# Three edits in a three-branch decoder kernel: weights loaded a phase ahead, gates projected transposed and kept on chip, the last mixer's loop interleaved

## The chip, the cores and the metric

The kernel runs on one core of one Trainium2 chip. The metric is the device time of one execution in microseconds (us), the median over runs.

## What is computed

The reference is one inference step of a two-layer recurrent decoder trunk, for 1024 prompt tokens and for 64 sample tokens (8 requests of 8 tokens, each with its own carried states), model width 1024, all in fp32. Layer 0 holds two mixers (a gated delta rule and an RWKV-7 scan), layer 1 an mLSTM with 8 heads (query and key width 64, value width 128). The change touches the input side of layer 0 and all of layer 1:

```
xn = rms_norm(x, norm1_w);  proj = xn @ w_in1          # q, k (512 each), v, o, z (1024 each), gates
pm  = exp(d - mt) * (q @ k.T)                          # masked decay times scores, per head
num = exp(inter - mt) * (q @ C) + pm @ v               # C, n: matrix memory and normaliser
den = exp(inter - mt) * (q . n) + sum(pm)
h   = num / max(|den|, exp(-mt))
C   = e_c * C + (w_s * k).T @ v;   n = e_c * n + sum(w_s * k)
y   = rms_norm(x + (h * sigmoid(o) * silu(z)) @ w_out1, norm_f_w)
```

Outputs are y for prompt and sample, and the final states of prompt and sample (the sample states have a leading dimension of 8).

## The kernel before

The program is written by hand: each phase is one block in which every engine has its own instruction stream, ordered by semaphores; a phase starts when the one before has ended on all engines. SP issues all DMAs, on one queue. Tokens are tiled by 128 (8 prompt tiles) with one more tile of 64 sample tokens. An fp32 product is made of three TensorE matmuls on split operands (`products`, L82: high times high, high times low, low times high), so every weight block is loaded to SBUF, its high part cast by ACT (`...h`), and its low part subtracted by POOL (`...l`).

The phases, with the prefix that their buffers carry in the trace:

- `phase_norm` (n_, L96): RMSNorm of all tiles, the result turned into x transposed (K.xh, K.xl).
- `phase_gdn_in` (a_, L289): SP loads its weights when the phase starts (L342 to L349), ACT casts (L440, L442), POOL subtracts (L400, L405); PE projects the gates and then 4 groups of 4 column blocks of 128, weights stationary and x moving in pieces of 364, 364 and 360 columns (THIRDS). `over` (L281) runs the body for column block 0, for 1 and 2 in a hardware loop, and for 3.
- `phase_rwkv_in` (b_, L677): the same for the second mixer; its first weights (L725) and parameters (L727 to L730) are loaded when it starts.
- `phase_mix0` (c_, L1053): both mixers of layer 0, the output projection, the next norm. The change leaves it alone.
- `phase_mlstm_in` (e_, L2113): input projection of layer 1 in 16 blocks of 256 columns. The 4 blocks of q and k have the weights stationary. The 12 blocks of v, o and z (L85 to L87 under the loop at L2407) have x stationary and 256 weight columns moving: 9 token tiles times 8 contraction pieces times 3 products, 216 matmuls a block. ACT and DVE make the gate sigmoid(o) * silu(z) in tile GO, and SP stores v, gate and the running maxima (L2209, L2210, L2222, L2223) to scratch in DRAM.
- `phase_mix1` (f_, L2425): one step for each token tile. On PE, in this order: decay logits broadcast to all partitions (L2796, contraction 8), q times k (L2802), decay of the state (L2807), k turned to rows (L2810); then, for the tile before, the gated rows H turned (`end_rows`, L2772) and the output projection of 48 matmuls of 512 columns (`end_project`, L85 to L87); then for this tile the numerators, which alternate two shapes head by head (L2825 pm times v with contraction 128, L2827 q times C with contraction 64), and the state update (`update`, L2763). DVE masks (L2664), multiplies and scales, multiplies H with the gate rows GR that SP loaded, updates C (L2735), adds the residual and norms. Tiles 0 and 1 are written out, 2 to 7 are a hardware loop, and the sample tile comes last, alone: its numerators need each request's own state (L2831, 64 matmuls), its update goes through 8 requests one after the other (`with_batches`), and SP stores each request's states (L2555, L2556). At the phase's start SP loads w_out in 8 pieces, which ACT casts (L2609) and POOL and DVE subtract (L2568, L2710), and while the second tile runs the sample states (L2534, L2535, 32 DMAs).

Of the kernel before, what the change touches and what calls it, by code (L numbers as in the profile page):

```python
# [95 lines left out]
def phase_norm(nc, K, x_prompt, x_sample, shift, norm_w, p_shift, s_shift):  # L96

    with ExitStack() as ctx:
# [13 lines left out]
        with nc.Block() as block:  # L112
            @block.sync
            def _(sp):
# [3 lines left out]
                with sp.Fori(0, TILES // 2 - 1) as g:  # L118
                    for b in range(2):
                        sp.wait_ge(norm, 2 * g + b + 1)  # L120
                        sp.dma_start(x[:, b, :], x_prompt[0, bass.ds((2 * g + b + 2) * P, P), :]).then_inc(x_in[b], 16)
# [167 lines left out]
def phase_gdn_in(nc, K, w_in, conv_w, conv_state, a_log, dt_bias, S, p_conv, s_conv):  # L289


    with ExitStack() as ctx:
        sb = lambda n, s: ctx.enter_context(nc.sbuf_tensor("a_" + n, s, F32))
        sem = Events(nc, ctx, "a_")
        W = [sb(f"w{m}", [P, KT, P]) for m in range(4)]
        parts = lambda n, s: [ctx.enter_context(nc.sbuf_tensor(f"a_{n}{h}", s, F32R)) for h in "hl"]
        WP = [parts(f"wp{m}", [P, KT, P]) for m in range(4)]
        wg = sb("wg", [P, KT, 2 * AH])
# [9 lines left out]
        rows = sb("rows", [64, AQKV])  # L308
# [5 lines left out]
        gp = sb("gp", [P, 2, AH])  # L314
# [20 lines left out]
        halo, tailed, tails_t, tails_kept, tails_out, par, par2, pre_t, pre_k, gates, gate_a, gate_v, padded, dseq, pseq = [sem(n) for n in (  # L335
            "halo", "tailed", "tails_t", "tails_kept", "tails_out", "par", "par2", "pre_t", "pre_k", "gates", "gate_a",
            "gate_v", "padded", "dseq", "pseq")]

        with nc.Block() as block:
            @block.sync  # L340
            def _(sp):
                sp.dma_start(W[0][:, :, :], w_block(w_in, 0, P)).then_inc(w_ld[0], 16)  # L342
                sp.dma_start(cw_rows[:, :], conv_w).then_inc(par, 16)
                sp.dma_start(cs_rows[:, :], conv_state.rearrange("b r c -> (b r) c")).then_inc(par, 16)
                sp.dma_start(wg[:, :, :], w_block(w_in, AGATE, 2 * AH)).then_inc(par, 16)
                sp.dma_start(gp[:, 0, :], as_row(a_log)).then_inc(par2, 16)
                sp.dma_start(gp[:, 1, :], as_row(dt_bias)).then_inc(par2, 16)
                for m in range(1, 4):
                    sp.dma_start(W[m][:, :, :], w_block(w_in, m * AKEY, P)).then_inc(w_ld[m], 16)  # L349

                def load(m, j):
                    sp.wait_ge(low[m], j + 1)
                    alone(sp, K)
                    sp.dma_start(W[m][:, :, :], w_block(w_in, m * AKEY + (j + 1) * P, P)).then_inc(w_ld[m], 16)

                def body(j, more):
                    for m in range(3):
                        if more:
                            load(m, j)
# [11 lines left out]
                    if more:  # L371
                        load(3, j)
# [15 lines left out]
            def _(pool):  # L388
# [21 lines left out]
                def body(j, more):  # L410
# [7 lines left out]
                    for m in range(3):  # L418
# [8 lines left out]
                        if more:  # L427
                            split(m, j + 1)
                    if more:
                        split(3, j + 1)  # L430
# [3 lines left out]
            def _(act):  # L434
                def split(m, j):

                    act.wait_ge(w_ld[m], 16 * (j + 1))
# [3 lines left out]
                act.wait_ge(par, 48)  # L441
# [12 lines left out]
                act.wait_ge(par2, 32)  # L454
# [40 lines left out]
                def body(j, more):  # L495
                    keep(0, j)
                    if more:
                        split(0, j + 1)
                    keep(1, j)
                    if more:  # L500
                        split(1, j + 1)
# [3 lines left out]
                    if more:  # L505
                        split(2, j + 1)
# [18 lines left out]
                    if more:  # L525
                        split(3, j + 1)
# [3 lines left out]
            def _(dve):  # L530
# [9 lines left out]
                dve.wait_ge(par2, 32)  # L540
# [57 lines left out]
            def _(pe):  # L598
                pe.wait_ge(par, 48)
# [74 lines left out]
                over(pe, AH, body)  # L674


def phase_rwkv_in(nc, K, w_in, mu, w0, w2, a0, a2, k_k, k_a, r_k, S):  # L677

    with ExitStack() as ctx:
# [40 lines left out]
        with nc.Block() as block:  # L722
# [58 lines left out]
            def _(act):  # L781
# [20 lines left out]
                for m in range(4):  # L802
                    split(m, 0)
# [2131 lines left out]
```

## Time and profile before

| | |
|---|---|
| median of 3 runs | 2180.28 us (2179.63 to 2193.6) |
| the profiled execution | 2189.03 us, its span 2187.2 us |
| mean granted TensorE clock | 0.907 of full |
| busy: PE / DVE / ACT / POOL | 1921.7 / 891.8 / 576.8 / 445.2 us |
| a_ phase, b_ phase | 72.5 to 308.7 us with its gates before, 308.7 to 607 us |
| c_ phase | 607 to 1378 us |
| e_ phase | 1378 to 1838.6 us |
| f_ phase | 1838.6 to 2187.2 us |

PE is TensorE's matmuls, PEld its weight loads, DVE VectorE, ACT ScalarE, POOL GpSimd, SPq the queue of SP. A matmul on fp32 operands leaves several records in the trace: an fp32 matmul of the f_ phase (numerators, scores) two, a product on split operands one each. PEclk is the granted TensorE clock as a share of full speed, 1.00 for 2.4 GHz and 0.50 for 1.2 GHz. A record's duration is that of one instruction from its start to its modelled end; consecutive matmuls overlap, so the pace is read from start to start.

### The profile page before, as it was taken

Reading aid. Unit: us, or ns where it says so; the run is one execution under the profiler, and the core shown is the slowest. Engines: PE = TensorE matmul, PEld = TensorE weight load, DVE = VectorE, ACT = ScalarE, POOL = GpSimd, SP = SyncE. Lnnn points to the kernel's source line nnn. Section 1 sums busy time; section 2 is a strip of 40 time slices with the busy share of each in tenths; the row PEclk is TensorE's granted clock in tenths of the full one; section 3 lists DMA queues with packets and bytes.
Section 4 is the critical chain, followed back from the end, with each engine's and each line's share of the span. In section 5 each row is a group of like instructions: output and inputs, shape, how many; then the busy total and the mean of one; then the engine's idle time right before and its main releaser. Section 6 shows DMA issues by size and latency. Waiting matters only on the chain. (4 is left out here: it accounts for less than half of the span.)

```text
span 2187.2 us, 33920 instructions
## 1 busy us (share of the span) xinstructions
PE 1921.7 (88%) x13387; PEld 1663.1 (76%) x13387; DVE 891.8 (41%) x1709; ACT 576.8 (26%) x1171; POOL 445.2 (20%) x444
## 2 busy tenths in 40 slices
PE   3999968999779999999999889499999996999985
PEld 2799858889668767776776666399999995777764
DVE  4255534655556546645654543320001102533432
ACT  4344432333323223323232112321111111211101
POOL 2322111112054234324333200221111110100000
PEclk9999989999879999999999786799999997688887
DMA  4122131331161112211231101522131113522215
GB/s 122 43 81 80 52 91 40 101 101 42 52 224 49 50 39 67 73 37 53 67 91 35 31 30 48 155 80 80 60 99 41 60 61 125 147 79 65 91 49 44
DMA packets 192189, 160.54 MB, mean 73 GB/s; under 512 B 34563, under 2 KB 174060, under 8 KB 192089
## 3 DMA queue, kind: packets, MB, share of 16 engines
q1 hardware_dynamic: 192088, 159.12, 25.1%
q8 instruction: 73, 1.20, 0.2%
q14 instruction: 28, 0.22, 0.0%
HBM read 103.96 MB, written 55.14 MB: 73 GB/s over the span
## 5 line engine op out<-in xcount | busy, mean ns | idle before, releaser
L1809 PE MATMUL c_banks<-c_wo,c_ot 128*128 128x512 f32 (+1 forms) x288 | 131.7, 612 | 0.5 <-ACT c_invt L1410 0.5
L2369 DVE SCALAR_TENSOR_TENSOR e_t<-e_t,e_bank 128x512 f32<-128x512 f32 (+1 forms) x20 | 12.7, 633 | 287.9 <-ACT e_t L2321 287.9
L85 PE MATMUL e_bank<-e_wp0h,e_xh 128*128 128x256 f32 x432 | 122.5, 283 | 1.5 <-issue 1.5
L85 PE MATMUL e_bank<-e_wp1h,e_xh 128*128 128x256 f32 x432 | 122.3, 283 | 0.0
L86 PE MATMUL e_bank<-e_wp1l,e_xh 128*128 128x256 f32 x432 | 122.3, 283 | 0.0
L87 PE MATMUL e_bank<-e_wp0h,e_xl 128*128 128x256 f32 x432 | 122.3, 283 | 0.0
L86 PE MATMUL e_bank<-e_wp0l,e_xh 128*128 128x256 f32 x432 | 122.3, 283 | 0.0
L87 PE MATMUL e_bank<-e_wp1h,e_xl 128*128 128x256 f32 x432 | 122.2, 283 | 0.0
L1350 POOL TENSOR_TENSOR c_m<-c_sc,c_lev 128x256 f32<-128x256 f32 (+1 forms) x118 | 97.7, 836 | 55.5 <-DVE c_sc L1657 52.8
L1809 PEld LDWEIGHTS c_banks<-c_wo,c_ot 128*128 128x128 f32 (+1 forms) x288 | 53.0, 189 | 67.5 <-issue 65.8
L1709 DVE TENSOR_TENSOR c_inv<-c_inv,c_banks 128x128 f32<-128x128 f32 (+1 forms) x252 | 59.0, 278 | 97.3 <-PE c_banks L1930 96.4
L1350 POOL TENSOR_TENSOR c_m<-c_nt,c_lev 128x256 f32<-128x256 f32 (+1 forms) x59 | 46.7, 792 | 252.7 <-DVE c_nt L1626 126.0
L85 PEld LDWEIGHTS e_bank<-e_wp0h,e_xh 128*128 128x128 f32 x432 | 82.9, 192 | 1.7 <-issue 1.7
L85 PEld LDWEIGHTS e_bank<-e_wp1h,e_xh 128*128 128x128 f32 x432 | 82.9, 192 | 0.0
L86 PEld LDWEIGHTS e_bank<-e_wp1l,e_xh 128*128 128x128 f32 x432 | 82.9, 192 | 0.0
L87 PEld LDWEIGHTS e_bank<-e_wp1h,e_xl 128*128 128x128 f32 x432 | 82.9, 192 | 0.0
L86 PEld LDWEIGHTS e_bank<-e_wp0l,e_xh 128*128 128x128 f32 x432 | 82.9, 192 | 0.0
L87 PEld LDWEIGHTS e_bank<-e_wp0h,e_xl 128*128 128x128 f32 x432 | 82.9, 192 | 0.0
L1908 PE MATMUL c_banks<-c_inv,c_m 128*64 128x64 f32 (+1 forms) x1008 | 60.5, 245 | 20.0 <-POOL c_m L1350 20.0
L1908 PEld LDWEIGHTS c_banks<-c_inv,c_m 128*64 128x64 f32 (+1 forms) x1008 | 42.7, 146 | 45.9 <-issue 30.1
L1930 PEld LDWEIGHTS c_banks<-c_y 64*128 64x128 f32 (+1 forms) x1008 | 67.7, 211 | 8.1 <-issue 8.0
L1930 PE MATMUL c_banks<-c_y 64*128 64x64 f32 (+1 forms) x1008 | 73.8, 300 | 0.0
(570 smaller groups left out, 5166.7 us busy)
## 6 DMA issues: line engine op xcount, KB each, us to landing
e_w<-in_w_in_dram SPq DMA_DIRECT2D x16, 1024.0 KB, 6.5
b_w<-in_w_in_dram SPq DMA_DIRECT2D x17, 512.0 KB, 6.4
scratch_rw<-b_x SPq DMA_DIRECT2D x16, 544.0 KB, 2.7
a_w<-in_w_in_dram SPq DMA_DIRECT2D x16, 512.0 KB, 5.8
c_rw<-scratch_rw SPq DMA_DIRECT2D x32, 256.0 KB, 2.9
scratch_qkv<-a_o SPq DMA_DIRECT2D x12, 544.0 KB, 4.7
e_xs<-scratch_xnT SPq DMA_DIRECT2D x8, 544.0 KB, 4.0
scratch_ql<-e_qb SPq DMA_DIRECT2D x8, 544.0 KB, 2.9
```

The source lines that it names most:

```text
L85: pe.matmul(out, w[0], x[0], start=first, stop=False)
L86: pe.matmul(out, w[0], x[1], start=False, stop=False)
L87: return pe.matmul(out, w[1], x[0], start=False, stop=last)
L1350: pool.tensor_tensor(M[u][0:T, :, 0:T // 2].rearrange("p k (b h) -> p k b h", h=1 << l), late(src, l, T), bc(lev[0:T, l:l + 1, 0:T // 2].r ...
L1709: dve.tensor_tensor(x, x, z, ALU.subtract).then_inc(ev(f"xd{u}"), 1)
L1809: mm = pe.matmul(bank[6 + c][0:T, :], OT[:, kt, 0:T], wo[:, kt, 512 * c:512 * c + 512], start=(kt == 0), stop=(kt == KT - 1))
L1908: mm = pe.matmul(y_at(u, T, k), M[u][0:T, k, 0:T // 2], half(X[u][0:T, k, :], l, T, 0), start=True, stop=True)
L1930: mm = pe.matmul(z_all(u, T, e)[:, p, :], XC[u][r, p, 0:T], Y[u][r, p, 0:T // 2], start=True, stop=True)
L2369: dve.scalar_tensor_tensor(out=t2, in0=t2, scalar=1.0, in1=two(b, at), op0=ALU.add, op1=ALU.mult).then_inc(ev(f"free{b}"), 1)
```

## The change

**Weights a phase ahead.** The weight and parameter buffers of a_ and b_ become shared ones (K.W, K.WP, K.rows, K.wg, K.gp, K.lora). a_'s are loaded by SP during `phase_norm`, between the x tiles. In the last column block of a_, SP loads b_'s first blocks into the same buffers, and ACT and POOL split them there; b_ projects its first blocks without a wait for weights.

```
                 sp.dma_start(x[:, n % 2, :], x_prompt[0, (n + 2) * P:(n + 3) * P, :]).then_inc(x_in[n % 2], 16)
+                if n == 1:
...
+                if n >= 2:
+                    sp.dma_start(K.W[n - 2][:, :, :], w_block(w_in0, (n - 2) * AKEY, P)).then_inc(K.a_w[n - 2], 16)
...
+                    if more:
+                        sp.dma_start(W[m][:, :, :], w_block(w_in, m * AKEY + (j + 1) * P, P)).then_inc(w_ld[m], 16)
+                    else:
+                        sp.dma_start(W[m][:, :, :], w_block(w_in, ACOLS + (m if m else 4) * BW, P)).then_inc(K.b_w[m], 16)
...
-                    if more:
-                        load(3, j)
+                    load(3, j, more)
```

The SP queue at the end of a_'s last column block, before, from the last store of q, k, v to b_'s first loads (a_z is the gate z, a_o are the projected columns, a_tails the last rows of the convolution):

```order
L362 DMA scratch_qkv<-a_o 128x1088
L367 DMA scratch_z<-a_z 128x8x128
L370 DMA scratch_z<-a_z 64x128
L376 DMA scratch_qkv<-a_o 128x1088 x2
L380 DMA out_p_conv_dram<-a_tails 9x1x128
L382 DMA out_s_conv_dram<-a_tails 72x1x128
L339 UNCONDITIONAL_BRANCH
L723 UNCONDITIONAL_BRANCH
L725 DMA b_w<-in_w_in_dram 128x8x128
```

and now:

```order
L358 DMA k_w<-in_w_in_dram 128x8x128 x3
L365 DMA scratch_qkv<-a_o 128x1088
L370 DMA scratch_z<-a_z 128x8x128
L373 DMA scratch_z<-a_z 64x128
L358 DMA k_w<-in_w_in_dram 128x8x128
L378 DMA scratch_qkv<-a_o 128x1088 x2
L382 DMA out_p_conv_dram<-a_tails 9x1x128
L384 DMA out_s_conv_dram<-a_tails 72x1x128
L343 UNCONDITIONAL_BRANCH
L720 UNCONDITIONAL_BRANCH
```

Three of b_'s first four blocks now stand ahead of a_'s last stores, the fourth behind those of z, and a_ ends only when it has been loaded and split.

**Gates transposed.** In e_, the 4 blocks of v come first, in the old form. The 8 blocks of o and z then have the weights stationary and x moving in THIRDS; the gate is written to K.G ([128, 8, 1088], transposed, on chip), so scratch g, tile GO, its stores and the loads of GR in f_ are gone. The stores of the running maxima move up behind the q and k blocks. Small buffers share space (QB lies on xs, li and lf on VB, bc_ is K.u).

```
-                with pe.Fori(0, ROUNDS) as g:
-                    for p in range(6):
+                with pe.Fori(0, V_BLOCKS // 2) as g:
...
+                with pe.Fori(0, OZ_BLOCKS // 2) as g:
+                    for p in range(2):
...
+                        for i in range(6):
+                            t, (at, n) = i // 3, THIRDS[i % 3]
+                            pe.wait_ge(ev(f"free{i}"), 2 * g + p + BEFORE_OZ[i])
+                            for kt in range(KT):
+                                w = [x[:, kt, t * P:(t + 1) * P] for x in WP[p]]
+                                mm = products(pe, bank[i][:, 0:n], w, [x[:, kt, at:at + n] for x in X], kt == 0, kt == KT - 1)
```

**The last mixer.** All loops of f_ are written out over 9 steps, and the sample tile is the fifth (`SLOT = 4`). In step k, PE does the numerators of k (8 matmuls pm times v, then 8 q times C), the update of k, half of the projection of k-1, the scores of k+1 (L2857 to L2872), the other half, and the turn of k. H is turned ungated; DVE multiplies by K.G behind the turn (`gate`, into OG), then ACT casts and DVE subtracts. XR, the residual rows, has two buffers; the first wait of DVE in f_, for the final norm's weights (`ld_nw`, loaded at L2528), moves behind step 0. The sample's numerators are 64 matmuls with contraction 64 in alternating row halves; its 8 request updates stand between the matmuls of the two projection halves, four in each. SP loads the sample states in 4 DMAs after step 0's loads and stores them in 8 DMAs in step 5.

```
+                scores(0)
+                for k in range(STEPS):
+                    numerators(k)
+                    if k != SLOT:
+                        pe.wait_ge(ev("og"), 2 * k)
...
+                        update(P, KW, EARLY, "upd")
...
+                    if k >= 1:
+                        project(k - 1, 0, early)
+                    if k + 1 < STEPS:
+                        scores(k + 1)
+                    if k >= 1:
+                        project(k - 1, 1, late)
+                    turn(k)
+                project(STEPS - 1, 0)
+                project(STEPS - 1, 1)
...
+                        if k == SLOT:
+                            sp.wait_ge(ev("upd_s"), DB)
+                        else:
+                            sp.wait_ge(ev("upd"), prompts(k + 1))
+                        load_v(k + 1)
...
+                    if k == SLOT + 1:
+                        store_states(0)
+                        store_states(DB // 2)
```

PE in a tile of f_ before (f_ut and f_et are decay rows, f_ql q and k, f_h the rows H, f_woh and f_wol w_out's parts, f_oth and f_otl those of the turned rows, f_va v, f_pm masked scores, f_c the state, f_kw scaled keys); the three projection rows stand 16 times, the two numerator rows 8 times:

```order
L2796 MATMUL f_bank<-f_ut,k_sel 128x128 x8
L2802 MATMUL f_bank<-f_ql 128x128 x8
L2807 MATMUL f_bank<-f_et,k_sel 128x128 x4
L2810 MATMUL f_bank<-k_ident,f_ql 128x128 x4
L2772 MATMUL f_bank<-k_ident,f_h 128x128 x8
L85 MATMUL f_bank<-f_woh,f_oth 128x512
L86 MATMUL f_bank<-f_wol,f_oth 128x512
L87 MATMUL f_bank<-f_woh,f_otl 128x512
...
L2825 MATMUL f_bank<-f_va,f_pm 128x129
L2827 MATMUL f_bank<-f_c,f_qe 128x129
...
L2763 MATMUL f_bank<-f_va,f_kw 64x129 x8
```

and now, from a step's numerators to its turn; the projection rows stand 8 times in each half:

```order
L2833 MATMUL f_bank<-f_va,f_pm 128x129 x8
L2839 MATMUL f_bank<-f_c,f_qe 128x129 x8
L2816 MATMUL f_bank<-f_va,f_kw 64x129 x8
L85 MATMUL f_bank<-f_woh,f_oth 128x512
L86 MATMUL f_bank<-f_wol,f_oth 128x512
L87 MATMUL f_bank<-f_woh,f_otl 128x512
...
L2857 MATMUL f_bank<-f_ut,k_sel 128x128 x8
L2862 MATMUL f_bank<-f_ql 128x128 x8
L2869 MATMUL f_bank<-f_et,k_sel 128x128 x4
L2872 MATMUL f_bank<-k_ident,f_ql 128x128 x4
...
L2883 MATMUL f_bank<-k_ident,f_h 128x128 x8
```

The numerators of one shape now stand together, the scores lie between two projection halves, and the turn is followed by numerators and update of the next tile rather than by the projection that needs its result.

## Rows read from the trace of the kernel before

**Rows 1.** Busy time by stage of e_ and f_: stretch, length, busy time and records of each engine, clock, DMA share.

```profile
1512.70:1838.60 325.90, 311.66 (x2596) 311.24 (x2594) 25.70 (x42) 52.99 (x71) 50.83 (x11) 0.98 0.20 62
...
1866.00:2081.00 215.00, 202.43 (x1016) 160.49 (x1015) 90.33 (x216) 32.39 (x91) 5.50 (x7) 0.81 0.31 89
2081.00:2108.30 27.30, 21.16 (x97) 16.09 (x97) 8.47 (x19) 3.27 (x14) 0.60 (x2) 0.87 0.18 58
2108.30:2171.50 63.20, 51.85 (x372) 40.54 (x372) 26.93 (x70) 8.06 (x19) 1.05 (x2) 0.77 0.34 44
2171.50:2187.20 15.70, 0.00 (x0) 0.00 (x0) 0.00 (x0) 0.00 (x0) 0.00 (x0) 0.50 0.81 46
```

**Rows 2.** PE in one tile of the f_ loop: start, length, engine, line, operands, records, [idle before].

```profile
1958.56 0.49 PE L2825 MATMUL f_bank<-f_va,f_pm 128*128 128x129 f32 x2
...
1958.98 0.49 PE L2827 MATMUL f_bank<-f_c,f_qe 64*128 64x129 f32 x2
...
1962.73 1.10 PE L2763 MATMUL f_bank<-f_va,f_kw 128*64 128x129 f32 x16
1963.77 2.05 PE L2796 MATMUL f_bank<-f_ut,k_sel 8*128 8x128 f32 x16
1965.74 1.16 PE L2802 MATMUL f_bank<-f_ql 64*128 64x128 f32 x16
1967.82 1.74 PE L2807 MATMUL f_bank<-f_et,k_sel 8*128 8x128 f32 x8 [0.92 <-DVE f_c L2735]
...
1970.58 1.94 PE L2772 MATMUL f_bank<-k_ident,f_h 128*128 128x128 f32 x8
...
1973.41 0.79 PE L85 MATMUL f_bank<-f_woh,f_oth 128*128 128x512 f32 x1 [0.89 <-DVE f_otl L2639]
...
1978.57 0.40 PE L85 MATMUL f_bank<-f_woh,f_oth 128*128 128x512 f32 x1
...
1986.97 0.38 PE L2825 MATMUL f_bank<-f_va,f_pm 128*128 128x129 f32 x2
```

**Rows 3.** The view of group 1, for pieces of that tile and the start of f_.

```profile
1968.10:1978.20 10.10, 9.21 (x31) 7.24 (x30) 5.49 (x14) 2.25 (x3) 0.00 (x0) 0.50 0.30 98
...
1838.60:1886.00 47.40, 38.50 (x157) 31.09 (x158) 23.23 (x44) 12.94 (x24) 10.92 (x6) 0.50 0.67 201
```

**Rows 4.** The timeline at the start of f_ and in its sample tile.

```profile
1849.99 2.16 DVE L2664 SCALAR_TENSOR_TENSOR f_dm<-f_bank,f_wt,k_lcausal 128x128 f32<-128x128 f32 x8 [22.80 <-DMA f_nw<-in_norm_f_w_dram]
...
2135.22 1.97 PE L2831 MATMUL f_bank<-f_cb,f_ws 128*64 128x129 f32 x16
```

**Rows 5.** The timeline at the end of e_.

```profile
1825.60 0.28 PE L87 MATMUL e_bank<-e_wp1h,e_xl 128*128 128x256 f32 x1
...
1838.69 0.41 SPq L2483 DMA_DIRECT2D f_ql<-scratch_ql  x1
```

**Rows 6.** PE in a_, eighteen moving matmuls of 364 and 360 columns apart.

```profile
285.95 0.32 PE L85 MATMUL a_bank<-k_xh,a_wp3h 128*128 128x364 f32 x1
...
288.93 0.33 PE L85 MATMUL a_bank<-k_xh,a_wp3h 128*128 128x360 f32 x1
```

**Rows 7.** The timeline from the norm to a_'s first product with weights.

```profile
46.47 0.43 SPq L342 DMA_DIRECT2D a_w<-in_w_in_dram  x1
...
53.12 0.26 ACT L442 ACTIVATE a_wgph<-a_wg 128x64 fp32r<-128x64 f32 x1 [8.84 <-DMA a_wg<-in_w_in_dram]
...
56.54 0.58 PE L85 MATMUL a_bank<-k_xh,a_wgph 128*8 128x512 f32 x1 [1.04 <-POOL a_wgpl L400]
```

**Rows 8.** The timeline from a_ to b_.

```profile
302.18 1.52 SPq L376 DMA_DIRECT2D scratch_qkv<-a_o  x2
...
308.82 0.41 SPq L725 DMA_DIRECT2D b_w<-in_w_in_dram  x1
...
312.80 1.06 ACT L801 ACTIVATE b_wp0h<-b_w 128x1024 fp32r<-128x1024 f32 x1 [13.68 <-DMA b_w<-in_w_in_dram]
...
316.42 0.64 PE L85 MATMUL b_bank<-k_xh,b_wp0h 128*128 128x364 f32 x1 [2.43 <-POOL b_wp0l L768]
```

More of the change, by code:

```diff
@@ L965, in project @@
                     b0 = 3 * (m % 2)
-                    pe.wait_ge(high[m], k + 1)
-                    pe.wait_ge(low[m], k + 1)
+                    if not (isinstance(k, int) and k == 0):
+                        pe.wait_ge(high[m], k)
+                        pe.wait_ge(low[m], k)
                     for g, (c, n) in enumerate(THIRDS):
@@ new lines, in _ @@
+                act.wait_ge(ev("turned"), 2)
+                for k in range(V0, OZ0):
+                    high(k + 1)
+                    act.wait_ge(ev("out_v"), 32 * (k - V0))
+                    for i, at in enumerate(PAIRS):
+                        b = V_PLACES[k % 2][i]
+                        r, n = at[2], slice(at[0], at[0] + at[1])
+                        act.wait_ge(ev("bank_full"), done_at(k, i))
+                        act.activation(VB[0:r, n, :], two(b, at), ACT.Copy).then_inc(ev(f"free{b}"), 1)
@@ L2683, in tile @@
+                    dve.wait_ge(ev("rows"), k + 1)
                     if T == P:
@@ new lines, in _ @@
+                dve.wait_ge(ev("ld_nw"), 16)
+                for k in range(STEPS):
+                    if k >= 2:
+                        add(k - 2, 1)
+                    if k >= 1:
+                        gate(k - 1)
+                    if k >= 2:
+                        scale(k - 2)
+                    if k >= 1:
+                        low(k - 1)
+                    if k >= 2:
+                        norm(k - 2)
+                    if k >= 1:
+                        rows_out(k)
+                        if k == SLOT:
+                            for b in range(DB // 2):
+                                states(b, EARLY)
+                        else:
+                            state(k)
+                        add(k - 1, 0)
+                    if k + 1 < STEPS:
+                        scores(k + 1)
+                    if k == SLOT:
+                        for b in range(DB // 2, DB):
+                            states(b, LATE)
@@ L2758, in _ @@
+                add(STEPS - 2, 1)
+                gate(STEPS - 1)
+                scale(STEPS - 2)
+                low(STEPS - 1)
+                norm(STEPS - 2)
+                add(STEPS - 1, 0)
+                add(STEPS - 1, 1)
+                scale(STEPS - 1)
+                norm(STEPS - 1)
             @block.tensor
@@ L2790, in tile, with sample_update @@
-                def tile(i, T, last):
-                    n = i + 1
-                    kept = i if T != P else i - 1 if not isinstance(i, int) or i > 0 else 0
-                    pe.wait_ge(ev("ut"), n)
-                    pe.wait_ge(ev("ot_low"), 2 * kept)
-                    for h in range(CH):
-                        mm = pe.matmul(v4(h // 4, T, T)[:, h % 4, :], K.sel[:, h, 0:T], ut[:, 0:T], start=True, stop=True)
+                def sample_update(b, banks):
+                    pe.wait_ge(ev("pick"), b + 1)
+                    if b % 4:
+                        pe.wait_ge(ev("cb"), b)
+                    update(SR, KM[b % 4], banks, "upd_s")
@@ L2797, in tile, with scores @@
+                def scores(k):
+                    T = order[k][2]
+                    pe.wait_ge(ev("ut"), k + 1)
+                    pe.wait_ge(ev("hr"), k)
+                    for h in range(CH):
+                        mm = pe.matmul(v4(6 + h // 4, T, T)[:, h % 4, :], K.sel[:, h, 0:T], ut[:, 0:T], start=True, stop=True)
                     mm.then_inc(ev("ub"), 1)
-                    pe.wait_ge(ev("hr"), i)
-                    pe.wait_ge(ev("ld_q"), 32 * n)
+                    pe.wait_ge(ev("ld_q"), 32 * (k + 1))
```

818 lines of the change are left out of this document (407 added, 411 removed).

## The prediction

> **What bounds the kernel now.** I read the busy time by stage first, then PE's timeline in one tile of the last mixer, then the seams between phases. In every long stage PE is the busiest engine: 311.7 of 325.9 us in e_, 202.4 of 215.0 us in the tile loop of f_, where DVE has 90.3 and ACT 32.4 us [rows 1]. So a step costs what PE needs for it, at the clock that it is granted. That clock is 0.98 of full in e_, but 0.81 in f_'s loop, 0.77 in its sample tile, and f_ ends with 15.7 us in which no engine works and only stores run [rows 1].
>
> One tile of f_ takes 215/7 = 30.7 us [rows 1]. By starts [rows 2]: numerators 16 pairs of records of 0.42 us, 6.7 us; update 1.04; scores 6.8, with a wait of 0.92 in it; turn 2.8, with a wait of 0.89; projection 13.56. From 1968.1 to 1978.2 the granted clock is 0.50 [rows 3], the lower of its two levels (1.2 GHz): it falls after the light scores and the first wait, and comes back only well inside the projection. From 1978.57 to 1986.97 the last 36 of its 48 matmuls take 8.40 us, 0.233 each; the 12 before took 5.16, 0.43 each [rows 2].
>
> **A, weights a phase ahead.** From the first load of a_ to the cast of its gate weights pass 53.12 - 46.47 = 6.65 us, and all behind that cast stays [rows 7]: at most 6.7 us are gained. The loads (four blocks of 0.5 MB, 2.1 MB) now run between the norm's x tiles; at the 201 GB/s of a stretch full of loads [rows 3] they need 10.4 us of DMA. If they held the norm for all of that, this would be a loss of 3.7; if they fit in its pauses, a gain of 6.7. I take +3. At the other seam, 316.42 - 308.82 = 7.6 us from b_'s first load to its first product go [rows 8]. But SP issues the fourth block's load behind z's stores, about 302; such a block is there 4.0 us after its issue (308.82 to 312.80), and cast and subtracted 3.6 us later (316.42) [rows 8]: about 309.5 to 311, and a_ ends behind that rather than at 308.8. I take +4 of 0 to 7.6. A: +7, between -4 and 14.
>
> **B, gates transposed.** The 12 blocks in the old form run from 1512.7 [rows 1] to 1825.88 [rows 5]: 26.1 us a block of 216 matmuls of 256 columns. A moving matmul of 364 columns takes (288.93 - 285.95)/18 = 0.1656 us [rows 6], so a block of 144 takes 23.8: 8 x 2.3 = 18 us, all of it on PE, which has no waits there (311.7 of 313.2 busy). The end of e_ is 1838.69 - 1825.88 = 12.8 us of two gate steps, the stores of gate and maxima and their landing [rows 5]; without stores I leave 2.8 us for the gate steps: +10 (bounds 5 and 12). The first block of v uses two banks that ACT and DVE have just filled into w and em: -1.5 (0 to -3). DVE's and ACT's work per block has the same number of elements, and has a block's 24 us to be done in. B: +26.5, between 20 and 29.
>
> **C, the last mixer.** A steady step of the new order, at full clock, from [rows 2]: turn 1.0 (1.94 at half clock); numerators 3.4; update 1.04; scores 1.97 + 1.16 + half of the 2.76 us that the decay and row matmuls take at half clock, 4.5, with 0.4 for hand-overs; projection 48 x 0.233 = 11.2; another 0.5 for hand-overs (between 0 and the 1.8 us of waits that the tile has now). Sum 22.0 us against 30.7.
>
> The numerators are the term that no row shows. Alternating the contraction 128 and 64, a record takes 0.21 us [rows 2]. Records of one shape take less: 1.97 us for the 16 of the sample's numerators, 0.12 each [rows 4], and 0.0725 for the scores in alternating row halves [rows 2], which is how the new q times C is laid out. So 16 x 0.12 + 16 x (0.0725 to 0.12) = 3.1 to 3.8, and 6.7 if grouping does nothing; I take 3.4, by the row of one shape.
>
> The Trainium skill, "TensorEngine Tiling (Array Packing)", section "Key Properties", says that changing the tiling mode, not only the tile, drains TensorE. By that rule the alternation pays at each of 16 switches and the grouped form at one or two; the 0.21 against 0.12 us agrees with it, and the sum would stay as it is.
>
> DVE does not become the bound: 90.3 us over 7 tiles is 12.9, ACT's 4.6 [rows 1]; even one after the other that is 17.5 of 22.0 us. What waits for what: the turn's result passes DVE (gate), ACT (high), DVE (low) while PE does the next tile's numerators and update (4.4 us), which is close; a shortfall of 0.5 is in the hand-overs. The masked scores are made under the second projection half (5.6 us).
>
> The steps, from [rows 1 to 4] where not said. Step 0: DVE's first mask waited until 1849.99 for the norm's weights [rows 4], 11 us into f_; that wait is gone and all behind it is some 6 us earlier, but the 8 casts of w_out and DVE's share of them still stand before step 1's scores, at half clock: 32.5. Step 1, cold with its first projection: 28. Steps 2, 3, 5, 6, 7: 5 x 22.0 = 110. Step 4: own numerators 1.9, 128 records of the states at 0.0725 to 0.12 (9 to 15, taken as 11), 8 updates of 1.04, projection 11.2, scores 4.9, turn 0.5: 38; then step 5 can load v only when the last update has read it, 4 us as for a block [rows 8]: 42. Step 8, without scores: 17. The end: gate, high, square, low with PE idle, a projection begun cold, add, norm, store: 26, nearly as the 27.3 us of the last prompt tile now [rows 1], since the store's landing is added and the next tile's part is not. Last, 3 us of low clock behind that 4 us wait, 3 for loads that queue behind the sample states' stores (15.7 us of stores at 0.81 of the DMA engines now [rows 1]), and 8 for some falls of the clock in the scores. Sum 32.5 + 28 + 110 + 42 + 17 + 26 + 14 = 269.5, against 2187.2 - 1838.7 = 348.5: +79. Bounds 45 and 105, by the rivals below.
>
> **Sum.** 7 + 26.5 + 79 = 112.5 us. The profiled execution took 2189.0 us (its span 2187.2 and 1.8 around it), so the same would read 2076.5. The median of the runs is 8.75 us lower, and the parts that differ are not in the edits: 2068 us.
>
> **Rivals.** First, the clock falls in every step (20%). For it: it does so in each tile now, after 4 us of light scores and a wait [rows 2, 3]. Against it: now 11 us of numerators, update and scores go before the fall, where the new order has at most 5.5 us between two halves of dense projection. Price: scores 1 us longer and the half behind them 2.4 us (12 matmuls at 0.43 rather than 0.233), 3.4 x 8 = 27, of which 8 are in the sum: 2087 us.
> The Trainium skill, "TensorE: Matmul & The Clock Gate", section "HAM oscillation — how this bites in real kernels", describes a kernel whose short bursts of matmuls are parted by gaps, and which starts each burst at the low clock. By that rule this rival would hold; the trace agrees so far for gaps behind light work [rows 2, 3] and does not show how it is without the gap.
>
> Second, all better (14%): no fall of the clock, no queueing, the wait for v hidden: 18 us of the 269.5 go, and the weights cost the norm nothing, 6 more: 2044 us.
>
> Third, grouping does nothing for the numerators (9%): 3.3 x 8 = 26: 2094 us. Against it stand the two faster rows above.
>
> Fourth, the hand-overs bind (6%): DVE, ACT and DVE between turn and projection take over 4.4 us, say 4 us more a step, 7 x 4 = 28: 2096 us. For it: three engines in a row, with the norm of an older tile in DVE's stream between them.
>
> Fifth, the other side (3%): the clock never comes up in f_. For it: in its first 47.4 us the granted clock is 0.50 although PE is busy for 38.5 of them [rows 3], and it is now dense projection of 13.6 us in one piece that raises it; halves of 5.6 us may not. A step at half clock is 2 x 21.5 + 0.5 = 43.5 us; seven of them 150 more and the sample 32 more, less the 14 above: 2068 + 168 = 2236 us. It decides once the clock stays down in more than six of the eight steps (134 us, the 112 gained and 1%, over 21.5 each).
>
> **How the numbers follow.** The forecast has 48%. A change of 1% (22 us) is about what a measurement of this kernel can tell from none. All cases but the fifth lie below 2158, and half clock in five or six steps would land near 2180: faster 0.96, same 0.02, slower 0.02. The range goes from 2036, with A and B at their upper ends on the second rival, to 2106, with the third or fourth rival and A at a loss; it leaves out the fifth and sums of two rivals.
>
> **What would show it.** Right: f_ of 255 to 285 us with steps of 21.5 to 24 us; numerators at 3.1 to 3.8 us; granted clock near 1.00 in the projection halves of steps 2, 3, 6, 7; no idle end of over 5 us; 23.8 us for a block of o or z; b_'s first product within 2 us of its phase's start, and a_ longer by 2 to 4. Wrong: a step of over 25 us, a clock of 0.5 in half of each step, the norm longer by over 5 us, or PE idle before the first projection half by more than 1 us in every step.

## The result, and the profile after

The changed kernel takes 2063.91 us, the median of 4 runs (2059.42 to 2072.46); the kernel before beside it took 2181.25 us. The ratio is 0.9446, with a 95% interval of 0.9412 to 0.948: 5.5% faster. The forecast was 2068, in a range from 2036 to 2106.

The profiled execution took 2063.12 us against 2189.03 before. Its busy times by phase (columns as in [rows 1]; the norm, a_, b_, c_, e_, f_, cut where each phase's first DMA is issued):

```profile
0.00:47.35 47.35, 16.24 (x72) 12.89 (x72) 23.92 (x37) 20.79 (x37) 13.44 (x47) 0.72 0.51 155
47.35:308.01 260.66, 232.89 (x1353) 213.49 (x1353) 121.81 (x143) 110.24 (x167) 62.25 (x64) 0.96 0.23 68
308.01:599.85 291.84, 253.06 (x1370) 236.40 (x1370) 150.56 (x137) 91.46 (x179) 35.23 (x18) 0.93 0.21 70
599.85:1365.76 765.91, 692.98 (x5778) 544.12 (x5778) 408.16 (x1004) 208.59 (x533) 235.57 (x277) 0.91 0.22 63
1365.76:1796.78 431.02, 407.93 (x2682) 400.93 (x2682) 57.42 (x75) 92.82 (x130) 80.62 (x24) 0.98 0.24 71
1796.78:2061.40 264.62, 233.21 (x1556) 191.80 (x1556) 134.78 (x326) 50.93 (x133) 19.73 (x15) 0.83 0.44 103
```

Against the same cuts of before (46.5, 262.4, 299.5, 769.3, 461.0, 348.5 us; c_ starts there with its first load at 608.3) the phases changed by +0.9, -1.7, -7.7, -3.4, -30.0 and -83.9 us: A 8.5 (forecast 7), B 30.0 (26.5), C 83.9 (79), and 3.4 in c_, which no edit touches.

The same view in finer pieces: the last two blocks of e_ work (v, then o and z), e_'s end, and in f_ step 0, steps 1 to 3, the sample's step 4, steps 5 to 7, step 8 with the final projection, and the last store:

```profile
1498.62:1602.40 103.78, 103.78 (x866) 103.78 (x865) 0.29 (x2) 18.01 (x23) 18.45 (x4) 1.00 0.28 79
1602.40:1794.20 191.80, 191.80 (x1154) 191.50 (x1152) 29.79 (x46) 35.23 (x55) 32.20 (x7) 1.00 0.13 39
1794.20:1796.78 2.58, 0.00 (x0) 0.00 (x0) 1.06 (x2) 0.47 (x1) 0.00 (x0) 1.00 0.00 0
1796.78:1831.12 34.34, 24.27 (x144) 21.58 (x145) 22.86 (x42) 12.14 (x21) 11.43 (x6) 0.58 0.92 263
1831.12:1895.09 63.97, 63.97 (x446) 53.61 (x445) 39.44 (x101) 11.05 (x37) 1.86 (x2) 0.96 0.39 99
1895.09:1938.81 43.72, 40.05 (x374) 32.14 (x373) 21.22 (x62) 10.25 (x23) 0.93 (x1) 0.88 0.07 22
1938.81:2018.79 79.98, 74.47 (x444) 60.07 (x445) 36.57 (x94) 11.46 (x37) 3.11 (x3) 0.81 0.63 108
2018.79:2057.20 38.41, 30.46 (x154) 24.41 (x152) 14.70 (x30) 6.02 (x15) 2.40 (x3) 0.88 0.15 48
2057.20:2061.40 4.20, 0.00 (x0) 0.00 (x0) 0.00 (x0) 0.00 (x0) 0.00 (x0) 0.50 0.31 127
```

The 8 blocks of o and z take 191.80 us, 24.0 each, where a block took 26.1 [rows 1, 5], and e_ ends 2.6 us behind its last matmul, not 12.8. In f_ the reader sees PE busy for 63.97 of 63.97 us in steps 1 to 3, with clock 0.96; then less in steps 4 to 7, where the clock is 0.88 and 0.81 and PE stands idle for 9 us. The idle end of 15.7 us [rows 1] is now 4.2.

One step, that of tile 2, on PE (as [rows 2]; L2883 is the turn, L2833 and L2839 the numerators, L2816 the update, L2857 to L2872 the scores; the projection halves stand where the lines are left out):

```profile
1852.14 1.03 PE L2883 MATMUL f_bank<-k_ident,f_h 128*128 128x128 f32 x8
1853.01 1.95 PE L2833 MATMUL f_bank<-f_va,f_pm 128*128 128x129 f32 x16
1854.89 1.16 PE L2839 MATMUL f_bank<-f_c,f_qe 64*128 64x129 f32 x16
1855.98 1.10 PE L2816 MATMUL f_bank<-f_va,f_kw 128*64 128x129 f32 x16
...
1862.81 2.05 PE L2857 MATMUL f_bank<-f_ut,k_sel 8*128 8x128 f32 x16
1864.78 1.16 PE L2862 MATMUL f_bank<-f_ql 64*128 64x128 f32 x16
1865.88 1.15 PE L2869 MATMUL f_bank<-f_et,k_sel 8*128 8x128 f32 x8
1866.96 0.87 PE L2872 MATMUL f_bank<-k_ident,f_ql 128*128 128x128 f32 x4
...
1874.63 1.04 PE L2883 MATMUL f_bank<-k_ident,f_h 128*128 128x128 f32 x8
1875.50 1.95 PE L2833 MATMUL f_bank<-f_va,f_pm 128*128 128x129 f32 x16
```

From 1853.01 to 1855.98 the numerators take 2.97 us, against 6.7 in [rows 2]: the 16 records of pm times v keep the pace of the sample's [rows 4], those of q times C that of the scores. The step is 22.5 us long. It has no wait, and yet two speeds: from the last records of the scores (row 1866.96) on, PE runs slower for a while. The granted clock around that place, and in the same place of step 7 (columns as before):

```profile
1862.81:1866.50 3.69, 3.69 (x38) 3.45 (x38) 2.30 (x8) 0.00 (x0) 0.00 (x0) 1.00 0.12 48
1866.50:1870.50 4.00, 4.00 (x16) 3.30 (x16) 3.20 (x8) 1.06 (x1) 0.00 (x0) 0.60 0.29 66
1870.50:1875.50 5.00, 5.00 (x26) 4.07 (x26) 0.60 (x1) 0.00 (x0) 0.00 (x0) 0.98 0.00 0
...
2006.54:2012.00 5.46, 5.46 (x32) 4.82 (x32) 4.08 (x13) 1.06 (x1) 0.00 (x0) 0.56 0.00 0
```

PE is busy in every microsecond of these windows. The clock falls inside the scores of step 7 and at the very end of those of step 2 (it stands at 0.50 from 1867.26 to 1870.67), and comes back inside the second projection half.

What PE waited for in steps 5 and 6, and SP's queue ahead of the second wait:

```profile
1938.81 3.69 PE L2833 MATMUL f_bank<-f_va,f_pm 128*128 128x129 f32 x16 [3.56 <-DMA f_va<-scratch_v]
...
1981.83 2.08 PE L2862 MATMUL f_bank<-f_ql 64*128 64x128 f32 x16 [5.51 <-DMA f_ql<-scratch_ql]
...
1956.14 5.91 SPq L2534 DMA_DIRECT2D out_s_n_dram<-f_cb  x1
1962.10 3.86 SPq L2532 DMA_DIRECT2D out_s_c_dram<-f_cb  x1
1965.99 4.80 SPq L2534 DMA_DIRECT2D out_s_n_dram<-f_cb  x1
1970.91 2.82 SPq L2497 DMA_DIRECT2D f_ql<-scratch_ql  x1
```

The first wait is for v behind the sample's last update, as forecast. The second is for q and k of the next tile: SP issued that load only at 1970.91, since the eight stores of the sample states, issued from 1946.9 on, took its time until then, some of them 4 to 6 us to issue.

The seams: a_'s first gate product (56.54 before [rows 7]), the cast of b_'s fourth block, and b_'s first product (316.42 before [rows 8]):

```profile
50.76 0.58 PE L85 MATMUL a_bank<-k_xh,a_wgph 128*8 128x512 f32 x1 [1.04 <-POOL a_wgpl L402]
...
297.93 1.04 SPq L358 DMA_DIRECT2D k_w<-in_w_in_dram  x1
...
303.42 1.06 ACT L445 ACTIVATE k_wp3h<-k_w 128x1024 fp32r<-128x1024 f32 x1 [8.54 <-DMA k_w<-in_w_in_dram]
...
308.28 0.67 PE L85 MATMUL b_bank<-k_xh,k_wp0h 128*128 128x364 f32 x1
```

### The profile page after: what moved, and what is told of

Same layout as the page of the kernel before. It is cut to its first block and busy times, and to the rows that moved or that the text cites. A ratio compares the mean times of both kernels' runs of the same rounds, so it can differ in the third digit from the quotient of the medians.

```text
span 2061.4 us, 32418 instructions
## 1 busy us (share of the span) xinstructions
PE 1836.3 (89%) x12811; PEld 1599.6 (78%) x12811; DVE 896.7 (43%) x1722; ACT 574.8 (28%) x1179; POOL 446.8 (22%) x444
## 5 line engine op out<-in xcount | busy, mean ns | idle before, releaser
L2368 DVE SCALAR_TENSOR_TENSOR e_t2m<-e_t2m,e_bank 128x364 f32<-128x364 f32 (+1 forms) x24 | 12.8, 532 | 265.1 <-ACT e_t2m L2320 265.1
L85 PE MATMUL e_bank<-e_xh,e_wp0h 128*128 128x364 f32 (+1 forms) x288 | 94.7, 329 | 3.6 <-POOL e_wp0l L2250 3.6
L86 PE MATMUL e_bank<-e_xl,e_wp0h 128*128 128x364 f32 (+1 forms) x288 | 94.6, 329 | 0.0
L86 PE MATMUL e_bank<-e_xl,e_wp1h 128*128 128x364 f32 (+1 forms) x288 | 94.6, 329 | 0.0
L87 PE MATMUL e_bank<-e_xh,e_wp0l 128*128 128x364 f32 (+1 forms) x288 | 94.6, 329 | 0.0
L87 PE MATMUL e_bank<-e_xh,e_wp1l 128*128 128x364 f32 (+1 forms) x288 | 94.6, 329 | 0.0
L85 PE MATMUL e_bank<-e_xh,e_wp1h 128*128 128x364 f32 (+1 forms) x288 | 94.5, 328 | 0.0
L2250 POOL TENSOR_TENSOR e_wp0l<-e_w,e_wp0h 128x2048 fp32r<-128x2048 f32 x8 | 36.8, 4595 | 159.1 <-ACT e_wp0h L2263 159.1
L2250 POOL TENSOR_TENSOR e_wp1l<-e_w,e_wp1h 128x2048 fp32r<-128x2048 f32 x8 | 38.7, 4837 | 147.2 <-ACT e_wp1h L2263 147.2
L85 PE MATMUL f_bank<-f_woh,f_oth 128*128 128x512 f32 (+1 forms) x144 | 63.9, 444 | 3.8 <-DVE f_otl L2677 3.8
L1445 ACT ACTIVATE c_y<-c_banks 128x128 f32<-128x128 f32 (+1 forms) x126 | 34.7, 275 | 111.2 <-PE c_banks L1900 110.3
L872 DVE TENSOR_TENSOR b_x<-b_u 128x1024 f32<-128x1024 f32 x16 | 19.6, 1224 | 96.4 <-ACT b_us L784 96.4
```

Source lines behind the costliest of these rows:

```text
L85: pe.matmul(out, w[0], x[0], start=first, stop=False)
L86: pe.matmul(out, w[0], x[1], start=False, stop=False)
L87: return pe.matmul(out, w[1], x[0], start=False, stop=last)
L1445: act.activation(Y[u][0:T, 0:2, 0:T // 2], y_all(u, T), ACT.Copy).then_inc(ev(f"y{u}"), 1)
L2250: pool.tensor_tensor(WP[b][1][:, :, :], W[b][:, :, :], WP[b][0][:, :, :].bitcast(F32), ALU.subtract).then_inc(ev(f"low{b}"), 1)
```

## The experiments

All are the changed kernel but for the edit shown; the ratio is to the kernel before, run beside each. The length of f_ is that of the profiled execution. Of the variants, the alternating numerators, the projection in one piece and the last two rows have a ratio clear of the changed kernel's interval; the others overlap with it. f_ alone scatters too: three profiles with the same code in f_ (changed, again, A undone) have 264.6, 273.4 and 267.3 us, most of the difference in one wait for q and k in step 6 (5.5, 13.1 and 11.1 us). So a smaller difference is read from the step in which it arises.

| run | ratio (95%) | f_, us |
|---|---|---|
| changed kernel | 0.9446 (0.9412 to 0.948) | 264.6 |
| changed kernel again | 0.9445 (0.9418 to 0.9473) | 273.4 |
| A undone | 0.9521 (0.9475 to 0.9567) | 267.3 |
| numerators alternate | 0.9598 (0.9568 to 0.9629) | 300.4 |
| projection in one piece | 0.9518 (0.9483 to 0.9552) | 282.1 |
| state stores spread | 0.9396 (0.936 to 0.9431) | 259.4 |
| scores cut up | 0.9496 (0.9464 to 0.9527) | 264.0 |
| step 0 of DVE turned | 0.9423 (0.9388 to 0.9459) | 259.4 |
| sample tile last | 0.9482 (0.9446 to 0.9519) | 266.1 |
| all edits | 0.9403 (0.935 to 0.9457) | 252.1 |
| all, cut up outside the sample only | 0.9315 (0.9293 to 0.9337) | 242.2 |
| the same, q times C first in step 5 | 0.9314 (0.929 to 0.9338) | 246.0 |

**A undone.** The three functions of the norm, a_ and b_ are put back.

> The norm, a_ and b_ phases are those of before; e_ and f_ are those of the changed kernel. If the early loads are worth what the seams show (a_'s first gate product at 50.8 rather than 56.5 us, b_'s first product at 308.3 rather than 316.4), c_ starts 8.5 us later than in the changed kernel and the time is 8 to 9 us longer, with f_ unchanged at about 264.6 us. Rival: the loads only move, what the seams gain is lost in the norm and at the end of a_; then under 3 us.

The ratio is 0.0075 higher, but the intervals touch, and in the profile c_, the same code, took 779.7 us rather than 765.9. By the phases, c_ starts at 604.0 us, against 599.9 in the changed kernel and 608.3 before, which runs the same code up to there. In the seven other runs with A as it is, c_ started between 598.4 and 600.3. So A is worth 4 to 10 us, and the rival falls; no closer, since the two executions without A differ by 4.3 us with the same code.

**Numerators alternate.**

```
-                    for h in range(CH):
...
+                        for h in (0, 2, 4, 6, 1, 3, 5, 7):
+                            r = slice(64 * (h % 2), 64 * (h % 2) + 64)
+                            pe.matmul(at(h), PM[0:T, h, 0:T], VA[0:T, h, :], start=h not in (2, 3, 4, 5), stop=False, skip_group_check=True)
+                            mm = pe.matmul(at(h), qe[r, h // 2, :], C[r, h // 2, :], start=False, stop=True, skip_group_check=True)
```

> The numerators of a prompt tile alternate head by head between contraction 128 and 64 again, all else as in the changed kernel. If the alternation itself costs (0.21 us a record against 0.09 in the grouped form), a step's numerators take 6.6 rather than 3.0 us: 3.6 us x 8 steps, 29 us longer, perhaps 2 to 3 less where they hide a wait. Rival: the grouped form is fast because nothing waits around it, not for its shape; then 0 to 5 us.

f_ is 35.8 us longer. The numerators of step 6 on PE, the first pair, the last record and the update behind it:

```profile
1994.96 0.39 PE L2837 MATMUL f_bank<-f_va,f_pm 128*128 128x129 f32 x2
1995.28 0.49 PE L2838 MATMUL f_bank<-f_c,f_qe 64*128 64x129 f32 x2
...
2001.13 0.49 PE L2838 MATMUL f_bank<-f_c,f_qe 64*128 64x129 f32 x2
2001.54 1.10 PE L2816 MATMUL f_bank<-f_va,f_kw 128*64 128x129 f32 x16
```

From 1994.96 to 2001.54 are 6.58 us, at full clock, for the same 32 records: 3.6 more a step, 29 in eight. Undoing the grouping brings the long numerators back. The edit also takes the heads in the order of before, so that four products q times C in a row lie in the same row half; what that alone costs was not run. Sixteen records of contraction 64 in one row half, the sample's pm times v in the changed kernel, take 1.98 us at full clock, 0.9 more than the 1.09 of q times C in alternating halves:

```profile
1895.09 1.98 PE L2833 MATMUL f_bank<-f_va,f_pm 64*64 64x129 f32 x16
```

So some 0.9 of the 3.6 us may be the order of heads (an estimate from these rows); the rest is the alternation of shapes. The other 7 us are the net of uneven steps: the sample's is 1.7 us shorter, and step 1 alone is 13.4 longer. Its busy time here, and in the changed kernel (columns as in [rows 1]):

```profile
1834.90:1870.20 35.30, 35.30 (x151) 27.41 (x150) 11.11 (x31) 3.23 (x11) 0.00 (x0) 0.66 0.37 73
...
1831.12:1853.01 21.89, 21.89 (x150) 18.60 (x150) 11.16 (x30) 3.23 (x11) 0.00 (x0) 0.95 0.60 119
```

Both steps begin at the low clock behind the idle time of step 0. With grouped numerators it comes up 1.0 to 4.1 us behind their start in step 1, in all eleven profiles that have them; with alternating ones only 17.4 us behind it, inside the projection's first half, though PE is busy throughout: 35.3 us at a mean clock of 0.66 against 21.9 at 0.95.

**Projection in one piece.**

```
                         project(k - 1, 0, early)
+                    if k >= 1 and k != SLOT:
+                        project(k - 1, 1, late)
                     if k + 1 < STEPS:
                         scores(k + 1)
-                    if k >= 1:
-                        project(k - 1, 1, late)
```

> In steps 1 to 3 and 5 to 8 both projection halves stand together before the scores of the next tile, as one piece of 11.2 us. My theory: the second half covers the chain mask 2.15, exp 1.06, masked scores 1.28, scaled keys 0.68 and their hand-overs, some 6 us behind the scores; without it the turn waits for the scaled keys, 5 to 6 us in each of 6 steps (the last has no scores): 30 to 36 us longer. Rival: the halves matter for the clock alone, which one long dense piece brings up better; then equal or up to 10 us shorter.

f_ is 17.4 us longer, its prompt steps 26.2 to 26.9 us; half of what I expected, and of the sign that the rival excluded. Numerators and turn of step 2:

```profile
1854.81 3.64 PE L2833 MATMUL f_bank<-f_va,f_pm 128*128 128x129 f32 x16
...
1879.65 1.94 PE L2883 MATMUL f_bank<-k_ident,f_h 128*128 128x128 f32 x8 [1.99 <-DVE f_kw L2734]
```

The wait is 1.7 to 2.0 us in the prompt steps, not 6 (5.5 in step 3, whose scores are the sample's): DVE's chain starts behind the first group of the scores, and the rest of them, 3.4 us here, covers its first half. What else the step lost is clock. It falls in the scores, and stays at 0.50 through the wait, the turn and the numerators behind it (pm times v 3.64 us rather than 1.95); before the change it stayed there through the turn and the first 12 matmuls of the projection. So the halves cover DVE's chain. That they also help the clock, by dense work soon behind the light, is argued from these rows and not shown by a run of its own.

**State stores spread.**

```
-                    if k == SLOT + 1:
-                        store_states(0)
-                        store_states(DB // 2)
+                    if k > SLOT:
+                        store_states((k - SLOT - 1) // 2 * (DB // 2), (k - SLOT - 1) % 2)
```

> The sample states are stored by one pair of DMAs in each of the steps 5 to 8, rather than by all eight in step 5. My theory: the wait of 5.5 us for q and k in step 6 is SP's queue standing behind those stores (24 us of issue); it goes, and with it part of the low clock behind it: 6 to 9 us shorter, and no wait of over 1 us for a load in steps 6 to 8. Rival: the stores' issue time only moves, and the last stores or a later load wait instead: no change, or longer at the end.

f_ is 5.3 us shorter, a little less than expected, step 6 takes 24.0 us rather than 30.3, and PE has no wait for a load in steps 6 to 8. The ratio is lower, but its interval overlaps with the changed kernel's. The stores' issue does not only move: in steps 6 and 7 a store now takes 0.8 to 1.2 us to issue, where it had taken up to 5.9. What the wait is worth differs by execution: it was 5.5 us in the changed kernel's profile and 13.1 in that of its repeat, where f_ took 273.4 us.

**Scores cut up.** The scores' function is split in three; the first part stays, the second goes behind 6 matmuls of the second half, the third behind 12.

> The scores no longer stand in one piece: their first group (decay logits, 2.0 us) stays between the projection halves, q times k goes behind the first 6 of the 24 matmuls of the second half, decay and rows behind the next 6. My theory: the clock falls in the piece of 4.8 us of matmuls of contraction 8 and 64; cut up it stays at full, and the four or five steps that fall in the changed kernel lose 3 us less each: 9 to 15 us shorter, prompt steps of 21 us. Rival: matmuls of contraction 8 and 64 let the clock fall wherever they stand, or each change of shape costs; then no change or up to 10 us longer.

f_ did not change, and the ratio is if anything worse. So I missed the total, but not for the rival's reason alone: steps 2, 5 and 7 took 21.3 to 22.9 us rather than 22.5 to 25.7, and steps 3 and 4, around the sample, lost it again with 22.8 and 48.6 rather than 19.6 and 43.7. Where the clock holds, cutting up costs 0.4 us a step (21.3 against the 20.9 below). Nor does it always hold: in steps 2, 5, 6 and 7 it fell from the scores on in 17 of the 20 steps of the five profiles with whole scores (changed, again, A undone, states spread, step 0 turned), and in 4 of the 16 of the four profiles with cut-up ones.

**Step 0 of DVE turned.** `scores(1)` goes ahead of the subtractions of w_out's pieces 5 and 7.

> In step 0 DVE makes tile 1's masked scores before its last two subtractions of w_out rather than behind them. My theory: the turn of step 0 waits 5.5 us for the scaled keys because DVE stands behind the casts; it goes 4 us earlier and all behind it: 4 us shorter. Rival: the first projection then waits for those two subtractions: no change.

f_ is 5.2 us shorter in the profile; the turn of step 0 waits 1.83 us instead of 5.47, and the first projection starts behind the update without a wait. In the ratio, 0.9423, so little cannot be told from none.

**Sample tile last.** `SLOT = 8`, the state stores behind the last prompt tile's.

> The sample tile is the last of the 9 steps rather than the fifth; its state stores stand at the end. My theory: its own work stays woven in either way; what the middle costs now is the wait of 3.6 us for v, that of 5.5 us for q and k behind the state stores and some 2 us of low clock behind them, 11 us; what the end would cost is some 10 us of state stores that nothing covers. So -5 to +8 us. Rival: the middle is worth the whole idle end of the kernel before, 15.7 us: 12 us longer or more.

+1.5 us in f_. No step waits for a load, and in steps 5 and 6 the clock holds; step 5, all of it:

```profile
1926.20:1947.12 20.92, 20.92 (x151) 17.64 (x150) 12.84 (x33) 4.18 (x13) 0.93 (x1) 1.00 0.32 102
```

What that gains goes into the stores at the end: the last of them is issued at 2044.61 and the sample's y behind it at 2047.73. The fifth place by itself is worth nothing measurable; with the stores spread, f_ is 7 us shorter than with the sample last.

**All edits.** States spread, scores cut up, step 0 turned, b_'s fourth block loaded ahead of z's stores, and DVE's subtraction ahead of the norm's scale at the end.

> States stored over steps 5 to 8, scores cut up, step 0 of DVE turned, b_'s fourth weight block loaded ahead of z's stores, and at the end the subtraction ahead of the norm's scale. If the causes add up: 5 (stores, measured) + 9 to 15 (clock) + 4 (step 0) + 2 (a_) + 1 (end) = 21 to 27 us shorter than the changed kernel. If the rival on the clock holds: 8 to 12.

f_ is 12.5 us shorter and a_ 2.7 us: 15 of the 21 to 27 us expected, more than the 8 to 12 of the rival. c_, unedited, was 10 us longer in this profile, and the runs lie between 2046 and 2069 us. PE's waits in the profile name what is left:

```profile
1903.50 1.06 PE L2890 MATMUL f_bank<-k_ident,f_h 128*128 128x128 f32 x8 [2.65 <-DVE f_kw L2734]
...
1939.68 1.98 PE L2817 MATMUL f_bank<-f_va,f_ws 64*64 64x129 f32 x16 [3.18 <-DVE f_cb L2765]
```

Behind the cut-up scores of the sample, the turn waits for DVE's scaled keys; in the sample's step its late updates wait for the states.

**Cut up outside the sample only.**

```
+                    whole = k in (0, SLOT - 1, SLOT)
+                    if whole:
+                        scores_qk(k + 1)
+                        scores_rest(k + 1)
```

> As the run with all edits, but the scores are cut up only in steps whose neighbours are prompt tiles: the sample's own scores and those made beside its late updates stand in one piece again. My theory: cut up, the rest of the scores comes late where DVE has the sample's four extra products to make or where the late updates take the places, and PE waits for the scaled keys; step 3 goes from 22.8 to 19.6 us and step 4 from 48.4 to 42 to 44, so f_ from 252 to about 244 us and the whole is 18 to 22 us below the changed kernel. Rival: those steps are long for the clock alone; then f_ stays at 250 to 253.

242.2 us in f_, and 2039.8 us in all beside 2068.2 of the changed kernel (2036 to 2043 against 2063 to 2079): 28 us less, with one more variant the best of this study, 6.9% below the kernel before. Step 3 took 19.6 us as expected, step 4 only came down to 45.4. No run has all the other edits with whole scores, so what cutting up gives by itself is read from the steps alone: steps 2, 5, 6 and 7 together took 86.6 us here and 95.0 with the states spread and whole scores. A prompt step on PE, between its numerators and the next, and its clock:

```profile
1842.90 1.95 PE L2834 MATMUL f_bank<-f_va,f_pm 128*128 128x129 f32 x16
...
1852.70 2.05 PE L2858 MATMUL f_bank<-f_ut,k_sel 8*128 8x128 f32 x16
...
1856.27 1.16 PE L2866 MATMUL f_bank<-f_ql 64*128 64x128 f32 x16
...
1858.95 1.15 PE L2876 MATMUL f_bank<-f_et,k_sel 8*128 8x128 f32 x8
...
1863.34 1.04 PE L2890 MATMUL f_bank<-k_ident,f_h 128*128 128x128 f32 x8
1864.21 1.95 PE L2834 MATMUL f_bank<-f_va,f_pm 128*128 128x129 f32 x16
```

```profile
1842.90:1864.21 21.31, 21.31 (x150) 17.47 (x149) 12.74 (x33) 4.17 (x13) 0.93 (x1) 1.00 0.29 87
1906.00:1920.00 14.00, 14.00 (x74) 10.92 (x75) 6.16 (x19) 1.06 (x1) 0.00 (x0) 0.54 0.01 1
```

21.31 us, all of it busy, at full clock; the step of the changed kernel that had the same work took 22.5 to 25.7. In the sample's step the clock still falls.

**q times C first in step 5.**

> As the run before it, but in the step behind the sample the 8 matmuls q times C stand ahead of the 8 pm times v, so that they run while v is loaded. They take 1.1 to 2.2 us: the wait of 3.6 us for v gets that much shorter, 1 to 2 us in all. Rival: the sample's last update is what ends last there, not the load; then nothing.

The wait for v is 1.99 rather than 3.75 us, as expected, steps 4 and 5 together took 67.1 rather than 68.1 us, and the time is the same: 2039.45 us. What it gains is under what the runs can tell: f_ is 3.7 us longer in this profile, in which the clock fell in steps 2 and 6, whose code is that of the run before.

**The changed kernel again.**

> The changed kernel again, as it is, to stand beside the two variants on one chip: its ratio to the kernel before is 0.941 to 0.948, f_ 262 to 267 us.

The ratio is as expected; f_ in the profile is 273.4 us, outside what I had written, mostly for the wait named above (7.6 us more of it). Its clock fell in step 1 as well (23.1 us), where the first profile had none.

## Why the prediction was right

The total was 112.5 us less by the forecast, 117.3 by the medians. Part of that closeness is luck. Profile against profile it was 125.9 us, 13.4 more than forecast: 1.5 in A, 3.5 in B, 4.9 in C and 3.4 in c_, which no edit touches. The profiled execution of before lies 7.8 us above the median of its runs, that of now 0.8 below, so the medians come closer to the forecast than the parts do. By the prediction's steps:

- **What bounds.** PE at its granted clock: steps 1 to 3 have no idle time on PE at all. The 0.5 us for hand-overs was too much; gate, cast and subtraction fit behind numerators and update, and the fourth rival, that they bind, has no row for it.
- **A.** The first seam gained 5.8 us at a_'s first product, the norm's 0.9 already taken off: +3 was low, for the loads fit into the norm's pauses (the norm took 45.9 to 47.5 us in the eleven executions with them, 45.5 and 46.5 without). The second gained 8.1 - 5.8 = 2.3 (forecast 4): the fourth block's load, issued at 297.93, was there 5.5 us later rather than 4.0, and a_ ended behind it. Loading it ahead of z's stores took 3 to 4 us more off a_ (256.7 to 257.9 in three runs, against 260.2 to 261.7). The mechanism was right, its two halves mis-sized in opposite directions.
- **B.** 8 x (26.1 - 24.0) = 17 of the 18 forecast, and 10.2 of 10 at the end. The 1.5 us of waiting for two banks did not come: v starts at 1498.62 with no wait. The rest is 0.6 us in the v blocks, and 1.5 in the q and k blocks and 0.8 at e_'s start, which no edit explains; in the q and k blocks of before the clock stood at 0.50 for 3.4 us (1415.21 to 1418.62), and now it does not. No run undoes B by itself: its account rests on these rows.
- **C, the steady step.** The forecast was 22.0 us at full clock. The runs show 20.9, where the clock does not fall (steps 5 and 6 with the sample last, step 2 with the stores spread). Numerators 2.97 (forecast 3.4, between 3.1 and 3.8), turn 0.9, update 1.0, hand-overs nearly nothing. That the numerators' old form costs 3.6 us a step is shown by undoing it, with the order of heads not parted from the shapes; of the four terms it was the one that no row of before held. "TensorEngine Tiling (Array Packing)" of the Trainium skill, section "Key Properties", says that a change of tiling mode drains TensorE; 6.58 against 2.97 us for the same matmuls at one clock agrees with it.
- **C, the other steps.** Step 0 took 34.3 (32.5), step 1 21.9 (28), step 4 43.7 (42), steps 2, 3, 5, 6 and 7 together 122.1 where 110 and a surcharge of 14 had been put, the end with step 8 42.6 (43). The 6 us of step 1 are the one term that was clearly wrong, and they are more than the whole difference in C, 4.9 us: I had let only the projection bring the clock up, as in [rows 2, 3], and the grouped numerators do it.
- **The surcharge** of 14 us fits in the sum because two errors offset each other. The five steps without it were put at 110, and are 4 x 20.9 and step 3, which makes the sample's shorter scores, at 19.6: 103. Over that they took 19 us: clock falls (8 us put, up to 3 us a step), low clock behind the wait for v (3 put, 1.7 seen in 3.69 against 1.95 us), loads behind the state stores (3 put, 5.5 to 13 measured: the issue of those stores was the mis-sized term, since the trace of before showed only their time at the end). Steps 5 and 6 took 25.7 and 30.3 us, by low clock in both and the wait for q and k in step 6. That is over the 25 that I had called a sign of being wrong, and the clock near 1.00 that I had named for the projection halves of steps 2, 6 and 7 did not come; the other signs went its way, the numerators a little below their range.
- **The rivals.** The first, that the clock falls in every step, was half true: it fell in steps 2 and 4 to 7, not in 1 and 3. Whether it needs a wait, the trace of before had left open; in step 2 it fell with none, behind matmuls of contraction 8 and 64. Those alone do not decide it, since the same order held the clock in step 1. The page "TensorE: Matmul & The Clock Gate" of the Trainium skill, section "HAM oscillation — how this bites in real kernels", tells of gaps between bursts; the rows above show the fall with PE busy for 4.00 of 4.00 us, so here the measurement decides. The second rival, no fall at all, is what the best variant's profile reaches in steps 2, 3, 6 and 7, and the next one's, with the same code there, in 3 and 7 alone. The third and the fifth fell.

Open is why the same order of matmuls keeps the clock in one step and loses it in another: with the sample last, steps 2 to 4 took 24.0 us and steps 5 and 6 20.9, with no wait in either. In each of steps 1, 2, 5 and 6 two executions of the same code in that step differed in this. Open too is c_, which took 765.8 to 779.7 us with the same code, its mean clock lower in the long ones.

## What to carry to other kernels

Try first to group matmuls by shape: alternating two contractions head by head cost up to 3.6 of 6.6 us a step here. Put short matmuls of small contraction between pieces of dense ones, where no chain of another engine waits for the last of them: around the sample this lost 3 to 5 us a step, elsewhere it gained up to 3. Put a dependent projection behind the next tile's independent work. Do not queue a burst of element-wise stores ahead of loads that the next step needs; spread it over the steps.

## What the runs showed that was not expected

The clock falls under unbroken work: PE busy throughout, clock 0.60 at the end of the scores and behind them in step 2, 0.56 from inside them in step 7. A store takes longer to issue in a row of others: those of the normaliser states took 0.9 to 1.8 us each when spread and up to 5.9 in a row. And the clock rose within 4.1 us of grouped numerators where it stayed at half for 17.4 us behind the same matmuls, alternating (0.95 against 0.66 over step 1).
